# Last stage of a two-block transformer kernel: four places for split weights and operands, three for products, loads of gates and gelus two pairs at a time

## What is computed

```python
def peer_ffn(h, w_q, keys1, keys2, u, v):
    ...
    # per token and head: 16 of 128 x 128 experts by their scores, with softmaxed gates
    ...
    # output: sum over the picked experts of gate * gelu(h . u[expert]) * v[expert]
```

## Time and profile before

| | |
|---|---|
| runs | 2816.53 us (median of 3; 2813.7 to 2821.87) |
| profiled execution | 2818.3 us, its span 2816.5 us |
| PE, DVE, ACT, POOL busy | 2587.7, 1667.6, 727.3, 1792.3 us |
| moved by DMA | 502.82 MB |
| last stage, first to last matmul | 2243.75 to 2810.56 us |

### The profile page before, as it was taken

How to read it: one execution, slowest core, us unless ns; L and a number is a source line. 1 busy time by engine, 2 the same in 40 slices (tenths; PEclk the granted TensorE clock), 3 DMA queues, 4 the chain that set the end, 5 groups by cost and what they waited for, 6 DMA issues and landing times.

```text
span 2816.5 us, 36632 instructions
## 1 busy us (share of the span) xinstructions
PE 2587.7 (92%) x12764; PEld 2166.2 (77%) x12764; DVE 1667.6 (59%) x3128; ACT 727.3 (26%) x1296; POOL 1792.3 (64%) x1315
## 2 busy tenths in 40 slices
PE   4989799999899998999989989999889999999998
PEld 2866578888586675677778889899889977777777
DVE  5447532111343325453459998778778387887888
ACT  4158320000222323433210011111112133323232
POOL 2746557767551243375646568888887688878775
PEclk8989899999998998999999999999999999999999
DMA  6224222222220021122222337887887699989996
GB/s 238 90 88 144 90 75 105 90 104 91 94 75 15 31 75 34 46 105 75 75 97 107 113 139 277 334 327 294 328 326 268 258 338 333 332 312 334 324 323 235
DMA packets 154451, 502.82 MB, mean 179 GB/s; under 512 B 11616, under 2 KB 78816, under 8 KB 122080
## 3 DMA queue, kind: packets, MB, share of 16 engines
q1 hardware_dynamic: 96432, 311.98, 31.4%
q0 software_dynamic: 36864, 134.23, 12.5%
q10 hardware_dynamic: 21040, 55.11, 5.1%
HBM read 448.84 MB, written 52.43 MB: 178 GB/s over the span
## 4 chain that ended last, share of the span: by engine, by line
PE 60%; DVE 13%; POOL 9%; DMA 9%; issue 4%; ACT 3%; SPq 0%; ACTq 0%; DVEq 0%; POOLq 0%
PE banks L545 8%; PE banks L547 8%; PE banks L546 8%; POOL W_lo L407 6%; DMA arena<-gates_dram 4%; PE banks L905 3%; PE banks L906 3%; PE banks L907 3%; PE banks L675 3%; PE banks L820 2%; PE banks L821 2%; PE banks L822 2%; DMA B_lo_plain<-u_rows,arena 2%; PE banks L693 2%; POOL W_hi L415 2%
## 5 line engine op out<-in xcount | busy, mean ns | idle before, releaser
L407 POOL TENSOR_TENSOR W_lo<-raw,W_hi 128x2048 fp32r<-128x2048 f32 x127 | 585.5, 4611 | 62.8 <-ACT W_hi L1319 57.4
L432 POOL TENSOR_TENSOR W_lo<-raw,W_hi 128x512 fp32r<-128x512 f32 x376 | 493.6, 1323 | 0.0
L435 POOL TENSOR_TENSOR beat<-zero 128x1 f32<-128x1 f32 x94 | 19.1, 204 | 651.0 <-PE banks L695 255.9
L820 PE MATMUL banks<-A_hi,W_hi 128*128 128x384 f32 x1024 | 383.0, 374 | 11.9 <-ACT B_plain L1257 9.8
L822 PE MATMUL banks<-A_hi,W_lo 128*128 128x384 f32 x1024 | 347.5, 339 | 0.0
L821 PE MATMUL banks<-A_lo,W_hi 128*128 128x384 f32 x1024 | 347.4, 339 | 0.0
L905 PE MATMUL banks<-W_hi,B_hi 128*128 128x512 f32 x768 | 305.6, 398 | 30.6 <-DVE B_lo L1828 30.6
L906 PE MATMUL banks<-W_hi,B_lo 128*128 128x512 f32 x768 | 303.9, 396 | 0.0
L907 PE MATMUL banks<-W_lo,B_hi 128*128 128x512 f32 x768 | 303.4, 395 | 0.0
L545 PE MATMUL banks<-A_hi,W_hi 128*128 128x512 f32 x680 | 265.9, 391 | 4.9 <-issue 4.9
L547 PE MATMUL banks<-A_hi,W_lo 128*128 128x512 f32 x680 | 264.9, 389 | 0.0
(11 more groups left out here) (259 smaller groups left out, 5514.0 us busy)
## 6 DMA issues: line engine op xcount, KB each, us to landing
raw<-weights SPq DMA_DIRECT2D x241, 1024.0 KB, 4.8
gelu_dram<-B_plain ACTq DMA_DIRECT2D x64, 384.0 KB, 6.4
gates_dram<-arena ACTq DMA_DIRECT2D x6, 4096.0 KB, 20.2
arena<-gelu_dram SPq DMA_DIRECT2D x64, 384.0 KB, 7.0
arena<-gates_dram SPq DMA_DIRECT2D x64, 384.0 KB, 10.3
W_plain<-weights SPq DMA_DIRECT2D x4, 1024.0 KB, 16.1
X<-x_t SPq DMA_DIRECT2D x1, 2048.0 KB, 14.6
arena<-v_rows,arena POOLq DMA_INDIRECT x128, 8.4
```

Source lines behind the costliest of these rows:

```text
L407: pool.tensor_tensor(W_lo[:, s % 2, :], raw[:, s % 2, :], W_hi[:, s % 2, :].bitcast(F32), ALU.subtract)\
L432: return pool.tensor_tensor(W_lo[:, j, cols], raw[:, j, cols], W_hi[:, j, cols].bitcast(F32), ALU.subtract)
L820: mm(to, lh, rh, start=k == 0, stop=False)
```

## The change

Split weights get four places (`v_hi`, `v_lo`: the two of `W_hi` and `W_lo`, and `B_hi` and `B_lo` as two more), operands four in `A_hi` and `A_lo`, which the stage before no longer needs. Products get three. ACT waits for outputs p-4 instead of p-2, and once for the stores of the gelus, whose source lies in `B_hi`. Gelus and gates are loaded for two pairs by one DMA each, in pieces of 1024 bytes for the gates, into two double places. DVE works two products ahead, and product p waits for low_of(p-3). SP's and PE's loops are written for four pairs at a time.

The diff, cut to its core:

```diff
-        gelu_in, g_in, prod = at(0, 2, 2 * TD), at(2048, 2, 2 * TD), at(4096, 2, 2 * TD)
+        gelu_in, g_in, prod = at(0, 2, 4 * TD), at(4 * 2 * TD, 2, 4 * TD), [at(16 * TD, 2 * TD), at(18 * TD, 2 * TD), at(16384, 2 * TD)]
...
+        v_first = (N_ADA + N_MID + PAIRS) % 2
+        v_hi = [W_hi[:, v_first, :], W_hi[:, 1 - v_first, :], *(B_hi[:, 4 * i:4 * i + 4, :].rearrange("p a b -> p (a b)")
+                                                                for i in range(2))]
+        v_lo = [W_lo[:, v_first, :], W_lo[:, 1 - v_first, :], *(B_lo[:, 4 * i:4 * i + 4, :].rearrange("p a b -> p (a b)")
+                                                                for i in range(2))]
...
-            def pair(s, j):
-                if isinstance(s, int):
-                    sp.wait_ge(g_stored[j], 8 * GB)
-                    sp.wait_ge(g_stored[1 - j], 8 * GB)
+            def two_pairs(s, d):
+                if s:
+                    sp.wait_ge(act_ready, s + 2 * d - 2)
                 else:
-                    sp.wait_ge(act_ready, s + (j - 1))
-                sp.wait_ge(gelu_stored[j], s * 8 + 16)
-                sp.dma_start(gelu_in[:, j, :], gelu_dram[s + j, :, :, :].rearrange("p i t -> p (i t)"))\
-                    .then_inc(pair_loaded[j], 16)
-                sp.dma_start(g_in[:, j, :].rearrange("p (q x) -> p q x", q=GB),
-                             g_dram[:, :, bass.ds(s * 2 + 2 * j, 2), :].rearrange("q p e t -> p q (e t)"))\
-                    .then_inc(pair_loaded[j], 16)
+                    for j in range(2):
+                        sp.wait_ge(g_stored[j], 8 * GB)
+                for j in range(2):
+                    sp.wait_ge(gelu_stored[j], s * 8 + (16 * d + 16))
+                sp.dma_start(gelu_in[:, d, :].rearrange("p (s x) -> p s x", s=2),
+                             gelu_dram[s + 2 * d:s + 2 * d + 2, :, :, :].rearrange("s p i t -> p s (i t)"))\
+                    .then_inc(pair_loaded[d], 16)
+                sp.dma_start(g_in[:, d, :].rearrange("p (q x) -> p q x", q=GB),
+                             g_dram[:, :, 2 * s + 4 * d:2 * s + 4 * d + 4, :].rearrange("q p e t -> p q (e t)"))\
+                    .then_inc(pair_loaded[d], 16)
             for j in range(2):
                 value_slab(0, j)
+            for d in range(2):
+                two_pairs(0, d)
             for j in range(2):
-                pair(0, j)
-            with sp.Fori(2, PAIRS - 1, 2) as s:
-                for j in range(2):
-                    value_slab(s, j)
-                    pair(s, j)
+                value_slab(2, j)
+            for s in range(4, PAIRS, 4):
+                for d in range(2):
+                    for j in range(2):
+                        value_slab(s, 2 * d + j)
+                    two_pairs(s, d)
...
-                    pool.wait_ge(v_half, s - (N_MID + PAIRS + 1))
-                    low_of(s)
+                    p = s - (N_MID + PAIRS)
+                    pool.wait_ge(v_half, p - 1)
+                    pool.tensor_tensor(v_lo[p % 4], raw[:, s % 2, :], v_hi[p % 4].bitcast(F32), ALU.subtract)\
+                        .then_inc(slab_split, 1)
...
-            def outputs_of(s, odd, final=False):
-                slot = (N_ADA + N_MID + PAIRS + odd) % 2
-                pe.wait_ge(slab_split, s + (odd + N_MID + PAIRS + 1))
-                pe.wait_ge(act_lo_ready, s + (odd + 1))
+            def outputs_of(s, i, final=False):
+                pe.wait_ge(slab_split, s + (i + N_MID + PAIRS + 1))
+                pe.wait_ge(act_lo_ready, s + (i + 1))
                 def part(q, half, j):
                     to = two_banks[q][:, 512 * half:512 * half + 512]
-                    lh, ll = act_tile("B", 4 + 2 * odd + j, P * q, P)
-                    rh, rl = w_tile(slot, D * j + 512 * half, 512)
+                    lh, ll = act_tile("A", 2 * i + j, P * q, P)
+                    cols = slice(D * j + 512 * half, D * j + 512 * half + 512)
+                    rh, rl = v_hi[i][:, cols], v_lo[i][:, cols]
...
-            with pe.Fori(0, PAIRS - 3, 2) as s:
-                for odd in range(2):
-                    outputs_of(s, odd)
-            outputs_of(PAIRS - 2, 0)
-            outputs_of(PAIRS - 2, 1, final=True)
+            with pe.Fori(0, PAIRS - 7, 4) as s:
+                for i in range(4):
+                    outputs_of(s, i)
+            for i in range(4):
+                outputs_of(PAIRS - 4, i, final=i == 3)
...
-            def high(s, j):
-                slab = s + (j + N_MID + PAIRS)
-                slot = (N_MID + PAIRS + j) % 2
-                act.wait_ge(slab_loaded[slot], s * 8 + (8 * (N_MID + PAIRS + j - slot + N_ADA - 4) + 16))
-                act.wait_ge(slab_used, slab - 1)
-                act.activation(W_hi[:, slot, :], raw[:, slot, :], ACT.Copy).then_inc(v_half, 1)
-            def operand(s, j):
-                act.wait_ge(act_ready, s + (j + 1))
-                if not isinstance(s, int):
-                    act.wait_ge(slab_used, s + (j + N_MID + PAIRS - 1))
-                act.activation(B_hi[:, 4 + 2 * j:6 + 2 * j, 0:TD], prod[:, j, :].rearrange("p (i t) -> p i t", i=2),
-                               ACT.Copy).then_inc(act_hi_ready, 1)
-            for j in range(2):
-                operand(0, j)
-            with act.Fori(2, PAIRS - 1, 2) as s:
-                for j in range(2):
-                    high(s, j)
-                    operand(s, j)
+            def high(p):
+                slab = p + N_MID + PAIRS
+                act.wait_ge(slab_loaded[slab % 2], 8 * (slab - slab % 2 + N_ADA - 4) + 16)
+                if p >= 4:
+                    act.wait_ge(slab_used, slab - 3)
+                act.activation(v_hi[p % 4], raw[:, slab % 2, :], ACT.Copy).then_inc(v_half, 1)
+            def operand(p):
+                act.wait_ge(act_ready, p + 1)
+                if p >= 4:
+                    act.wait_ge(slab_used, p + N_MID + PAIRS - 3)
+                act.activation(A_hi[:, 2 * (p % 4):2 * (p % 4) + 2, 0:TD],
+                               prod[p % 3].rearrange("p (i t) -> p i t", i=2), ACT.Copy).then_inc(act_hi_ready, 1)
+            for i in range(2):
+                act.wait_ge(gelu_stored[i], 8 * PAIRS)
+            for p in range(2):
+                operand(p)
+            for p in range(2, PAIRS):
+                high(p)
+                operand(p)
...
-                j = p % 2
-                dve.wait_ge(pair_loaded[j], 16 * (p - j) + 32)
-                dve.tensor_tensor(prod[:, j, :].rearrange("p (i q t) -> p i q t", i=2, q=GB),
-                                  gelu_in[:, j, :].rearrange("p (i q t) -> p i q t", i=2, q=GB),
-                                  g_in[:, j, :].rearrange("p (q i t) -> p i q t", i=2, q=GB), ALU.mult)\
-                    .then_inc(act_ready, 1)
+                d, j = p // 2 % 2, p % 2
+                dve.wait_ge(pair_loaded[d], 32 * (p // 4) + 32)
+                if p >= 3:
+                    dve.wait_ge(act_lo_ready, p - 2)
+                dve.tensor_tensor(prod[p % 3].rearrange("p (i q t) -> p i q t", i=2, q=GB),
+                                  gelu_in[:, d, 2 * TD * j:2 * TD * j + 2 * TD].rearrange("p (i q t) -> p i q t", i=2, q=GB),
+                                  g_in[:, d, :].rearrange("p (q i t) -> p i q t", i=4, q=GB)[:, 2 * j:2 * j + 2, :, :],
+                                  ALU.mult).then_inc(act_ready, 1)
             def low_of(p):
-                j = p % 2
                 dve.wait_ge(act_hi_ready, p + 1)
-                dve.tensor_tensor(B_lo[:, 4 + 2 * j:6 + 2 * j, 0:TD], prod[:, j, :].rearrange("p (i t) -> p i t", i=2),
-                                  B_hi[:, 4 + 2 * j:6 + 2 * j, 0:TD].bitcast(F32), ALU.subtract)\
-                    .then_inc(act_lo_ready, 1)
+                tiles = slice(2 * (p % 4), 2 * (p % 4) + 2)
+                dve.tensor_tensor(A_lo[:, tiles, 0:TD], prod[p % 3].rearrange("p (i t) -> p i t", i=2),
+                                  A_hi[:, tiles, 0:TD].bitcast(F32), ALU.subtract).then_inc(act_lo_ready, 1)
...
+            for p in range(2):
+                product_of(p)
             for p in range(PAIRS):
-                product_of(p)
-                if p == 2:
+                low_of(p)
+                if p + 2 < PAIRS:
+                    product_of(p + 2)
+                if p == 1:
                     dve.wait_ge(x_rows_ready, 1)
-                if p >= 2:
-                    add_rows(p - 2)
-                low_of(p)
-            for p in range(PAIRS - 2, PAIRS):
-                add_rows(p)
+                if p >= 1:
+                    add_rows(p - 1)
+            add_rows(PAIRS - 1)
```

## The result

| | before | after |
|---|---|---|
| median of four runs each, us | 2819.2 (2813.7 to 2825.62) | 3091.98 (3091.01 to 3093.42) |
| ratio, 95% interval | | 1.0968 [1.0954, 1.0983] |
| span of the profiled execution, us | 2816.5 | 3090.6 |

The change makes the kernel 9.7% slower, where 10.6% (3115 us) had been forecast. All of it lies in the last stage.

What follows compares the result with a forecast made beforehand. The prediction took a ring of waits through POOL, SP and DVE to bound the changed last stage: 27.7 us per two pairs. Start 2264.6, 29 laps, 40.7 and 5.9 give span 3114.5, predicted 3115 us (10.6% slower), range 3050 to 3190.

Steps and rivals of the forecast that it cites:

- The ring: Last stage: split, load, product, additions, gathers, split, gathers, split across POOL, SP, DVE; 27.7 us per two pairs; 0.86.
- The load term: Lap's link from split's end until slab, gelus and gates of two pairs land: 10.3 us, bounds 8.9 to 12.9.
- The estimate of 8.0 us: Load of 2.62 MB by the skill's fit, 2.0 us plus bytes / 436 GB/s; lap 25.6, total about 3052 us.
- The other terms: Lap without load: product 0.9, additions' start to W_lo 4.4, W_lo 4.6, second gathers 2.9, W_lo 4.6 us.
- The sum: Start 2264.6, plus 29 laps of 27.7 to 3067.9, plus 40.7 and tail 5.9: span 3114.5 us.
- PE's idle time: PE in the last stage idles some 10 us a lap: 27.7 less 16.3, less 1.6 for slow matmuls.
- Product of even pairs waits some 9 us: On DVE, every even pair's product waits some 9 us for the gates load, every odd pair's for none.
- What PE can win: Last stage: 567 us against 522 at full pitch, so at most 45 us, 1.6% of the time.
- Rival 1: No ring, only depth: gathers and splits run free of the additions, no stall, 2774 us; chance 0.03.
- rival 2: PE's clock stays at 1.2 GHz through a lap's matmuls, two pairs take 30.7 us, total 3205 us; chance 0.07.
- rival 3: Load at its upper bound, 12.9 us: lap 30.3, time 3193 us; within the ring's 0.86, no separate chance.
- rival 4: Nothing changes, gain and ring cancel; needs a lap of 17.8 us, a load of 0.4; about even 0.02.

Runs made afterwards that it cites:

- The two fastest kernels: Changed kernel with pairs' load ahead of the slabs, plus rows before the product (2775.6 us) or gathers one pair later (2774.7 us).
- the swapped kernel: Kernel before, two places, with gelus and gates of pair p issued ahead of slab p in SP's loop: 2779.6 us, ratio 0.9855 to the kernel before.
- the two cuts: Changed kernel with DVE adding rows of p-1 before product p+2 (2978.1 us), or with POOL's gathers issued one pair later (2956.1 us).
- both cuts: Changed kernel with two pairs loaded ahead of the slabs and DVE's rows before the product: 2775.6 us, ratio 0.9836 to the kernel before.

## Why the prediction was right, point by point

- **The ring, right.** The lap holds the links named, in their order, two slabs a lap, and 29 laps fill the stage. Cutting it in either of two places took the links out of the lap (and made the load longer); moving the load ahead of the slabs brought the time back.
- **The load term, 10.3 us: too long by 0.7.** This is the term that was mis-sized: 9.56 us in the mean, 9.81 in the lap shown. Where the 0.7 lies is read from the loads of the kernel after, between 2300 and 3000 us (KB each, median us from issue to landing), and from its slabs, shortest, median and longest:

```profile
raw<-weights SPq DMA_DIRECT2D x52, 1024.0 KB, 4.8
arena<-gelu_dram SPq DMA_DIRECT2D x26, 768.0 KB, 6.5
arena<-gates_dram SPq DMA_DIRECT2D x26, 768.0 KB, 8.7
```

```profile
DMA to landing us min/median/max: 4.7/4.8/5.0
```

  They are issued 0.03, 0.48 and 0.90 us behind the split's end, so they land some 4.8, 7.0 and 9.6 us behind it. The sum put the slab at 0.2 + 2.1 + 3.2 = 5.5 us (1.05 MB at 330 GB/s are 3.2); it lands after 4.8 every time, the very figure of the fastest slab in the earlier trace rows. Most of the 0.7 is this: a fixed part had been worked out with 395 GB/s and was then added to a time at 330. For the gelus and gates behind it the 330 GB/s held: 1.57 MB in 4.7 us are 334 GB/s, in the mean of all laps the gelus at 375 (2.1 us) and the gates, in pieces of 1024 bytes, at some 305 (2.6 us). The estimate of 8.0 us by the fit of the Trainium skill ("DMA: Bandwidth & Descriptors", section "Anatomy of one DMA — SWDGE (gpsimd) path") came out too short by 1.5; the page gives that fit for one DMA that GpSimd issues, while these are three that SP issues, so this case doesn't test it.
- **The other terms, right:** product 0.87 (0.9), additions' start to the split 4.37 (4.4), split 4.58 and 4.63 (4.6), second round of gathers 2.92 (2.9).
- **The sum.** 29 laps × 0.78 us too much are 22.6 us, nearly all of it the load term; the start was 2263.8 instead of 2264.6, and from split(61) to the span's end it took 46.0 us instead of 46.6. Together 24.0 us, the difference of the spans, 3114.5 to 3090.6. The errors have one sign, so the hit is not owed to errors that cancel.
- **PE's idle time, 10 us a lap forecast, 8.0 measured** (247.7 us in 31 stops): the lap is shorter, and ten slow matmuls a lap (6 to 14) cost 2.1 us, not 1.6. Neither is in the ring. The "about 8 per stall" was one stall's count: 12 stalls of 1.6 us would be 19 us, not the 14 that were left over. In the kernel before, seven of the 12 stops have slow matmuls behind them, 59 in all (12 us), the other five none.
- **Product of even pairs waits some 9 us: wrong.** It waits 16.4 us. I had counted from the load's issue (9.8 us), but DVE has nothing to do from the end of low_of on, 6.7 us before that issue.
- **What PE can win, at most 45 us: right to 3 us.** The two fastest kernels are 47 and 48 us under the kernel before in their own measurement. But it was put down as the worth of the places, and that is not shown: the places alone give 17 us, and the swapped kernel 40 without them.
- **Rival 1** (no ring) is refuted by the two cuts, **rival 2** (slow clock bounds) by matmuls at 0.227 us in every lap, **rival 3** (load at 12.9 us) by the load term of 9.6, and **rival 4** (no change) by the time. The DMA share in the stage, 0.63 in the stretch shown, is as forecast (0.6).

## What to carry to other kernels

Where several queues wait on each other, write down each ring of waits, with how many steps of the loop one lap advances, and divide: the change turned 22.8 us for three slabs into 26.9 us for two, with no link of the ring longer than before. It only holds one split and one round of gathers more, for a slab less. A transfer that has its own buffers free should not stand in a queue behind one that waits for something else; in the kernel before, putting the light load ahead of the waiting one was worth 40 us, the added places alone 17. A wait in the list of waits does not show that its link bounds, nor does an engine that is busy 98.7% of the time; cutting it does.

## What was not expected of the hardware

- A load's price depends on what else is let go with it: the same 2.62 MB took 9.6 us alone and 12.2 to 12.3 us beside gathers (means of all laps), so a cut of 6.6 us took only 3.9 off the lap.
- Pieces of 1024 bytes seem to cost the DMA engines less time: at 355 GB/s their share is 0.94 with both cuts, and 1.00 at 351 GB/s in the swapped kernel, which loads gates in pieces of 512 bytes. Those loads are also half as many and twice as large, and no run parts the two.
- How many slow matmuls follow a stop of PE is not told by the stop's length. In the kernel before there are ten stops of 2.8 us in the last stage. Behind seven of them stand 6 to 14 matmuls at 0.427 us (9 behind the one of the earlier trace rows), in two of these cases only after another 1 to 1.5 us at full pitch; behind the other three none. This is one of those (timeline of the kernel before); from there on the starts are 0.23 to 0.24 us apart:

```profile
2357.54 0.50 PE L905 MATMUL banks<-W_hi,B_hi 128*128 128x512 f32 x1 [2.80 <-DVE B_lo L1828]
2357.87 0.40 PE L906 MATMUL banks<-W_hi,B_lo 128*128 128x512 f32 x1
```

  In the kernel after there are 6 to 14 behind each of its 31 stops.
